# Feed-forward gate and up products by Strassen's scheme, with the down projection as a second phase

## What is computed

```python
def swiglu(h, wg, wu, wd):
    return (jax.nn.silu(h @ wg) * (h @ wu)) @ wd

x = x + g_m * rmsnorm(y, p['norm_mix_post'][l])          # y: the mixer's output projection
h = rmsnorm(x, p['norm_ffn_pre'][l]) * (1 + sc_f) + sh_f
f = swiglu(h, p['w_ffn_gate'][l], p['w_ffn_up'][l], p['w_ffn_down'][l])
x = x + g_f * rmsnorm(f, p['norm_ffn_post'][l])
```

## Time and profile before

| | |
|---|---|
| runs, us | 3237.58, 3239.43, 3239.88 (median 3239.43) |
| span of the profiled execution, us | 3236.1 |
| instructions | 63340 |
| busy share PE / PE weight load / DVE / ACT / POOL | 93% / 84% / 47% / 30% / 33% |
| DMA | 278.56 MB, mean 86 GB/s |
| tail of layer 0 | from 1042 to about 2036 us |
| tail of layer 1 | from 2273 us to the end |

### The profile page before, as it was taken

How to read it: one execution, slowest core, us unless ns; L and a number is a source line. 1 busy time by engine, 2 the same in 40 slices (tenths; PEclk the granted TensorE clock), 3 DMA queues, 4 the chain that set the end, 5 groups by cost and what they waited for, 6 DMA issues and landing times. The chain is left out here.

```text
span 3236.1 us, 63340 instructions
## 1 busy us (share of the span) xinstructions
PE 3020.7 (93%) x25847; PEld 2727.6 (84%) x25847; DVE 1534.6 (47%) x2856; ACT 958.8 (30%) x1871; POOL 1052.5 (33%) x693
## 2 busy tenths in 40 slices
PE   6999899889998989999999998898889999999997
PEld 4878576555556989999999997887889999999997
DVE  4332255555555573333333348787373333333336
ACT  5411146321112442111111126666452111111123
POOL 2410167433332532211212215675533112112212
PEclk8999989888889999999999999999999999999999
DMA  9555200355554222111111113201332111111103
GB/s 317 170 175 199 74 21 1 126 184 177 184 177 138 89 88 65 40 45 39 42 49 45 45 36 95 77 23 29 94 96 68 44 45 45 39 39 52 41 25 104
DMA packets 243842, 278.56 MB, mean 86 GB/s; under 512 B 13770, under 2 KB 191307, under 8 KB 243396
## 3 DMA queue, kind: packets, MB, share of 16 engines
q1 hardware_dynamic: 221500, 196.01, 19.4%
q0 software_dynamic: 20992, 75.51, 7.0%
q10 hardware_dynamic: 1168, 4.46, 0.4%
HBM read 249.69 MB, written 24.26 MB: 85 GB/s over the span
## 5 line engine op out<-in xcount | busy, mean ns | idle before, releaser
L564 PE MATMUL ps<-HS,w_ring 128*128 128x272 f32 x4992 | 643.4, 290 | 15.5 <-PEq L156 12.1
L564 PEld LDWEIGHTS ps<-HS,w_ring 128*128 128x128 f32 x4992 | 635.3, 189 | 16.8 <-POOLq L1071 12.3
L564 PE MATMUL ps<-HS,w_split 128*128 128x272 f32 x4608 | 593.0, 290 | 9.5 <-POOL w_split L1009 9.5
L564 PEld LDWEIGHTS ps<-HS,w_split 128*128 128x128 f32 x4608 | 587.1, 189 | 11.6 <-issue 7.6
L572 PE MATMUL ps<-hid,w_ring 128*128 128x272 f32 x4224 | 551.1, 291 | 3.5 <-DVE hid L1242 2.9
L572 PEld LDWEIGHTS ps<-hid,w_ring 128*128 128x128 f32 x4224 | 537.9, 189 | 7.6 <-DVE hid L1242 3.4
L1009 POOL TENSOR_TENSOR w_ring<-w_raw,w_ring 128x1024 fp32r<-128x1024 f32 x92 | 220.5, 2408 | 831.9 <-ACT w_ring L707 831.9
L1319 DVE TENSOR_TENSOR Y<-Y,ps 128x272 f32<-128x272 f32 x576 | 252.2, 438 | 176.7 <-PE ps L572 176.7
L1233 DVE TENSOR_TENSOR sg<-sg,ps 128x272 f32<-128x272 f32 x176 | 76.5, 437 | 382.4 <-ACT sg L818 382.3
L1853 PEld LDWEIGHTS ps<-HS_in,w_split 128*128 128x128 f32 x1728 | 222.2, 191 | 27.7 <-issue 16.4
L1853 PE MATMUL ps<-HS_in,w_split 128*128 128x272 f32 x1728 | 233.1, 293 | 9.2 <-DVE HS_in L2072 9.1
(11 more groups left out here) (413 smaller groups left out, 3882.2 us busy)
## 6 DMA issues: line engine op xcount, KB each, us to landing
w_mod_half<-w_mod_in SPq DMA_DIRECT2D x40, 1024.0 KB
w_raw<-w_ffn_gate_in SPq DMA_DIRECT2D x44, 512.0 KB
w_raw<-w_ffn_up_in SPq DMA_DIRECT2D x44, 512.0 KB, 3.7
w_raw<-w_ffn_down_in SPq DMA_DIRECT2D x44, 512.0 KB, 3.5
x_part<-x_spill SPq DMA_DIRECT2D x58, 272.0 KB, 2.9
x_spill<-Y SPq DMA_DIRECT2D x12, 1088.0 KB, 5.6
w_raw<-w_in_ab_in SPq DMA_DIRECT2D x18, 512.0 KB
w_raw<-w_in_cd_in SPq DMA_DIRECT2D x14, 512.0 KB, 3.9
```

The lines of the kernel that those rows point to most:

```text
L564: ins = pe.matmul(bank(b), wt[:, a, k, :], HS[:, e, k, qs(q)], start=(k == 0 and j == 0), stop=(k == KD - 1 and j == 2))
```

## The change

The token quarters are taken in two pairs (0 with 1, 2 with 3) and the 1024 features in two halves. For a pair, a hidden group of 256 columns and one matrix (gate or up), the product is a 2 x 2 by 2 x 2 block product, done in Winograd's form of Strassen's scheme: seven block products of 4 x 3 = 12 matmuls (`strassen`), called a unit, in place of the eight that four calls of `product` amount to.

- Weights: for each group and matrix, a batch, both column tiles arrive as two raw halves of 512 KB (`load_parts`). DVE makes four sums in place (`part_sum`), ACT seven high parts (`part_high`), POOL seven low parts (`part_low`), each 128 x 512. There is one slot for each part.
- Tokens: sums and differences of the blocks of `h` are made in `Y` in place (`token_sum`), and split like before (`token_high` on ACT, `token_low` on DVE), seven parts for each pair.
- Out of PSUM: a copy by ACT (`copy_a`), five additions by DVE (`add_b`, `add_e`, `add_22`, `add_12`, `add_21`), then the four sigmoids or high parts, multiplications and, for up, low parts.
- Order: groups 0 to 2 run on pair 0 alone, groups 3 to 10 on both pairs, then groups 0 to 2 on pair 1: 28 batches, 44 units. The work that the first loop did beside the first group (`first_beside`) lies beside units 0 to 6.
- Hidden activations, high and low, are stored to a DRAM scratch `hid_spill` (`store_hid`) and read back into `HS` (`load_hid`, `load_last`). The down projection runs after all units: four chunks of four hidden rows of 128 (12 matmuls for each of 32 banks), then a last one of six rows, quarter by quarter (18 matmuls), with the post norm beside it. The loops are written out.

In the units' code `u` is a unit, `m` its batch, `soon` that it is a batch's last unit and the batch has two, `late` that the batch has one. The diff, cut to the parts that set the order (`G` are three buffers of 272 columns, `finish` a sigmoid or a high part):

```diff
+KH = KD // 2
+SOLO = 3
+NCHUNK = 4
+DOWNS = 32 * NCHUNK
+NPROD = 7
+
+
+HALF_JOBS = ([(f, (0,)) for f in range(SOLO)] + [(f, (0, 1)) for f in range(SOLO, NFG)] + [(f, (1,)) for f in range(SOLO)])
+HALF_BATCH = [(f, mat, pairs) for f, pairs in HALF_JOBS for mat in range(2)]
+HALF_UNIT = [(m, f, mat, n) for m, (f, mat, pairs) in enumerate(HALF_BATCH) for n in pairs]
...
+DOWN_ROWS = [2 * f + i for c in range(NCHUNK) for f in (SOLO + 2 * c, SOLO + 2 * c + 1) for i in range(2)]
+DOWN_ROWS += [2 * f + i for f in range(SOLO) for i in range(2)]
...
+        def part_from(j):
+
+            low, high = slice(0, P), slice(P, 2 * P)
+            if j == 2:
+                return s1[:, :, :]
+            u, cols = {0: (0, low), 1: (0, low), 3: (1, low), 4: (0, high), 5: (1, low), 6: (1, high)}[j]
+            return part_raw[u][:, :, cols]
...
+        def load_hid(eng, k):
+
+            for i in range(4):
+                if i % 2 == 0:
+                    eng.wait_ge(hid_out, 32 * U.hid_stored(DOWN_ROWS[4 * k + i] // 2, (0, 1)))
+                base = 2 * Q * (k % 2)
+                src = hid_spill[DOWN_ROWS[4 * k + i]].rearrange("p a (h t) -> p a h t", h=2)
+                for a in range(2):
+                    eng.dma_start(HS[:, a, 2 * i:2 * i + 2, base:base + 2 * Q].bitcast(F32), src[:, a]).then_inc(hid_in[k % 2], 16)
...
+            def load_parts(m):
+                f, mat, pairs = U.BATCH[m]
+                src = w_cols((wg_d, wu_d)[mat], f * FG, FG)
+                if m == 0:
+                    sp.wait_ge(w_lo, 7)
+                else:
+                    sp.wait_ge(part_lo, NPROD * m)
+                for u in range(2):
+                    sp.dma_start(part_raw[u], src[:, KH * u:KH * u + KH, :]).then_inc(part_in[u], 16)
...
+            def store_hid(u):
+                m, f, mat, n = U.UNIT[u]
+                sp.wait_ge(hid_lo, 4 * U.ups(u) + 4)
+                dst = hid_spill[2 * f:2 * f + 2].rearrange("f p a t -> p a f t")[:, :, :, 2 * Q * n:2 * Q * n + 2 * Q]
+                for a in range(2):
+                    sp.dma_start(dst[:, a], hid[:, a].bitcast(F32)).then_inc(hid_out, 16)
...
+            def load_down(t):
+                if t < 2:
+                    sp.wait_ge(part_lo, NPROD * NBATCH)
+                else:
+                    sp.wait_ge(down_lo, t - 1)
+                apart(sp, sp_passed)
+                sp.dma_start(raw[t % 2][:, :], wd_d[DOWN_ROWS[t] * P:(DOWN_ROWS[t] + 1) * P, :]).then_inc(down_in[t % 2], 16)
...
+            for u in range(END):
+                m, f, mat, n = U.UNIT[u]
+                if u == U.FIRST[m] and m + 1 < NBATCH:
+                    load_parts(m + 1)
+                if u == 1:
+                    store_x(0, 3)
+                if u >= 1 and U.UNIT[u - 1][2]:
+                    store_hid(u - 1)
...
+            def strassen(u, j):
+
+                m, f, mat, n = U.UNIT[u]
+                b = (0, 1, 2, 0, 1, 2, 1)[j]
...
+                if j < 3 and u < 2:
+                    pe.wait_ge(freed_act, 4 * KD - NB6 + 3 * u + j + 1)
+                elif j == 0:
+                    pe.wait_ge(muls, 4 * (u - 2) + 1)
+                elif j == 1:
+                    pe.wait_ge(taken, 5 * (u - 2) + 5)
+                elif j == 2:
+                    pe.wait_ge(taken, 5 * (u - 2) + 4)
+                elif j == 3:
+                    pe.wait_ge(a_copied, u + 1)
+                else:
+                    pe.wait_ge(taken, 5 * u + j - 3)
+                pe.wait_ge(part_lo, NPROD * m + j + 1)
+                if u in (0, U.BOTH):
+                    pe.wait_ge(h_lo, NPROD * n + TOKEN_AT[j])
+                for k in range(KH):
+                    for i, (a, e) in enumerate(((0, 0), (0, 1), (1, 0))):
+                        ins = pe.matmul(psum(U.banks(u)[b]), part_slot(j, a)[:, k, :], token_part(n, j, e)[:, k, :],
+                                        start=(j < 3 and k == 0 and i == 0),
+                                        stop=(j in (3, 5, 6) and k == KH - 1 and i == 2), skip_group_check=True)
+                ins.then_inc(prod, 1)
+
...
+            for u in range(END):
+                for j in range(NPROD):
+                    strassen(u, j)
...
+            for k in range(NCHUNK):
+                pe.wait_ge(down_lo, 4 * k + 4)
+                pe.wait_ge(hid_in[k % 2], 128 * (k // 2 + 1))
...
+            def part_high(m, j):
+                if m == 0:
+                    act.wait_ge(computed, U.mix((3, 4, 4, 5, 5, 6, 6)[j], 3) + 1)
+                else:
+                    act.wait_ge(prod, NPROD * U.LAST[m - 1] + j + 1)
+                if j in (0, 3, 6):
+                    act.wait_ge(part_in[0 if j == 0 else 1], 16 * m + 16)
+                else:
+                    act.wait_ge(sums_made, 4 * m + {2: 1, 4: 2, 1: 3, 5: 4}[j])
...
+            def copy_a(u):
+                act.wait_ge(prod, NPROD * u + 1)
+                if u >= 1:
+                    act.wait_ge(muls, 4 * u)
+                act.activation(G[0], psum(U.banks(u)[0]), ACT.Copy).then_inc(a_copied, 1)
...
+            def half(u):
+                m, f, mat, n = U.UNIT[u]
+                more = u == U.LAST[m] and m + 1 < NBATCH
+                soon = more and not U.alone(m)
+                late = more and U.alone(m)
+
+                def finish(i):
+                    if mat:
+                        hidden_high(u, i)
+                    else:
+                        sigmoid(u, i)
+
+                copy_a(u)
+                if m and u == U.FIRST[m] and U.alone(m - 1):
+                    part_high(m, 5)
+                    part_high(m, 6)
+                first_beside(u, 0)
+                if soon:
+                    part_high(m + 1, 0)
+                    part_high(m + 1, 1)
+                    part_high(m + 1, 2)
+                    if mat:
+                        part_high(m + 1, 3)
+                        part_high(m + 1, 4)
+                finish(0)
+                first_beside(u, 1)
+                if late:
+                    part_high(m + 1, 0)
+                if soon and not mat:
+                    part_high(m + 1, 3)
+                first_beside(u, 2)
+                finish(1)
+                first_beside(u, 3)
+                if soon and not mat:
+                    part_high(m + 1, 4)
+                finish(2)
+                if late:
+                    part_high(m + 1, 1)
+                    part_high(m + 1, 2)
+                finish(3)
+                if late:
+                    part_high(m + 1, 3)
+                    part_high(m + 1, 4)
+                if soon:
+                    part_high(m + 1, 5)
+                    part_high(m + 1, 6)
+                first_beside(u, 4)
...
+            def down_high(t):
+                act.wait_ge(down_in[t % 2], 16 * (t // 2) + 16)
+                if t < 3:
...
+            for t in range(4):
+                down_high(t)
+            act.wait_ge(prod, NPROD * END)
+            load_hid(act, 1)
+            for t in range(4, 10):
...
+            def part_low(m, j):
+                pool.wait_ge(part_hi, NPROD * m + j + 1)
+                pool.tensor_tensor(part_slot(j, 1), part_from(j), part_slot(j, 0).bitcast(F32), ALU.subtract
+                                   ).then_inc(part_lo, 1)
...
+            def down_low(t):
+                w = slots[DOWN_SLOT[t]]
+                pool.wait_ge(down_hi, t + 1)
+                pool.tensor_tensor(w[:, 1, :], raw[t % 2][:, :], w[:, 0, :].bitcast(F32), ALU.subtract).then_inc(down_lo, 1)
...
+            def part_sum(m, j):
+                a11, a21 = part_from(0), part_from(4)
+                a12, a22 = part_from(3), part_from(6)
+                if j == 2:
+                    if m == 0:
+                        dve.wait_ge(computed, U.mix(3, 3) + 1)
+                    for u in range(2):
+                        dve.wait_ge(part_in[u], 16 * m + 16)
+                    ins = dve.tensor_tensor(s1[:, :, :], a21, a22, ALU.add)
+                elif j == 4:
+                    ins = dve.tensor_tensor(a21, a11, a21, ALU.subtract)
+                elif j == 1:
+                    dve.wait_ge(part_lo, NPROD * m + 1)
+                    dve.wait_ge(sums_made, 4 * m + 1)
+                    ins = dve.tensor_tensor(a11, s1[:, :, :], a11, ALU.subtract)
+                else:
+                    dve.wait_ge(part_lo, NPROD * m + 4)
+                    dve.wait_ge(sums_made, 4 * m + 3)
+                    ins = dve.tensor_tensor(a12, a12, a11, ALU.subtract)
+                ins.then_inc(sums_made, 1)
...
+            def add_b(u):
+                dve.wait_ge(prod, NPROD * u + 2)
+                dve.wait_ge(a_copied, u + 1)
+                dve.tensor_tensor(G[1], G[0], psum(U.banks(u)[1]), ALU.add).then_inc(taken, 1)
+
+            def add_e(u):
+                dve.wait_ge(prod, NPROD * u + 3)
+                dve.tensor_tensor(G[2], G[0], psum(U.banks(u)[2]), ALU.add).then_inc(taken, 1)
...
```

(37 more changed lines are left out.)

1332 lines of the change are left out of this document (706 added, 626 removed).

## The result

The changed kernel takes 3370.7 us (median of 4 runs, 3370.2 to 3371.3) and the kernel before 3239.6 beside it: ratio 1.0408, 95% interval 1.0393 to 1.0423, slower by 131 us. The forecast was 3361. The profiled execution has a span of 3369.1 us, 133.0 more than before.

A forecast was written before the change was run, and what follows sets the result against it. It took PE's matmul count to bound the kernel. Removed matmuls -132.6, supply loop +181, first units and mixer +24, double units +28, hidden-activation loads +6, hand-over +33, last quarters -18: +121.4, device time 3361 us, range 3200 to 3440.

The forecast's parts named there:

- matmuls removed: Gate and up products in both tails: 528 fewer matmuls a tail at 0.1256 us, -66.3 us each, -132.6 for two.
- mixer's last quarter: End of the mixer, DVE having 25 us of work beside 24 of PE: +2 us a tail.
- double units: Units while batches serve both token pairs: late sum 5 delays the next unit's `add_b` in up batches, +28 us in all.
- hand-over: From PE's last unit product to the down phase: waits for four low parts of weights, +16.5 us a tail, +33.
- last quarters: Last part of the down phase, now four even blocks of 18 us without sigmoids: -9 us a tail, -18.
- The supply loop: Units serving one pair: load waits for the previous batch's low parts; 18.8 us against 10.55, 22 times, +181.
- The shared access: DVE and POOL block each other on SBUF's shared ports: 2.3 us of the 18.8 us loop.
- Token work beside the first units: DVE and ACT token operations in each tail's first units, half hidden in the load wait: +10 us a tail.
- first rival: In units serving one pair, the reload is hidden well enough: loop 15.3 us, 3212 us total; chance 0.15.
- third rival: In units serving one pair, the loop runs at PE's pace because the load is early: 3180 us; chance 0.05.
- The slow clock: Stalls keep PE's clock low through units serving one pair: loop 21 us and more, 3447 us; chance 0.12.

The follow-up runs named there:

- The reorder: The mixer's third and fourth row sums issued later on PE, on the kernel where DVE makes low parts 3 and 6; ratio 1.0045 to the kernel before.
- the control: The changed kernel measured again, unaltered, on the chip of the follow-up runs; ratio 1.0420 to the kernel before, +132.0 us.

## Why the prediction was right, and where its sizes were off

Tail 0 by the prediction's own terms (stretches above, less 10.55 us a unit; before's stretches in the same way):

| term | predicted | measured |
|---|---|---|
| matmuls removed | -66.3 | -66.3 (by count) |
| units 0 to 6, less the 15.0 us that before lost in its first groups | +59.5 | +58.7 |
| last six units | +41.3 | +43.5 |
| mixer's last quarter | +2 | +12.1 |
| double units, `load_hid(0)` in them | +17 | +9.2 |
| hand-over | +16.5 | +16.0 |
| last quarters | -9 | -7 |
| sum | +61 | +66.2 |

**The bound and the matmuls.** Right where PE is fed. The run with the matmuls put back shows that in the single units they have no price, which the sum took in from the other side: it set each such unit at the loop's length.

The total is nearer than its terms. The two largest misses of a tail, +10.1 in the mixer and -7.8 in the double units, nearly cancel, and that is luck.

**The supply loop.** Right in its size: 18.4 us a unit late, for 18.8. The runs show the two things that it was built from, the load (4.7 and 3.9 us, priced 3.9) and the serial chain behind the landing. One step of that chain is missing from the prediction. It has sum 5 wait for low part 3; but sum 5 stands on DVE behind `add_b`, and in nine of the eleven single turns of tail 0 it starts straight behind `add_b`, 0.7 to 3.4 us after that low part is made. `add_b` waits for PE's second product, which takes 3.06 us at the slow clock in the turn shown, and for DVE's own queue (there four low parts, 4.73 us for 4 x 0.44 alone). No run parts the two. Nor are the chain's parts independent: of the three orders that start some of them earlier, two are slower beyond their intervals and none is faster.

**The shared access.** The sum priced it at 2.3 us a loop. The row of sum 5 beside POOL (1.27 for 0.68 us, so 0.6 of wait where the sum had 1.1) and 1.9 us a unit without that sum do not speak against it. The other way round it was priced too low: the four low parts of an up unit stand 4.73 us on DVE for 1.76 alone. The Trainium skill (SBUF — State Buffer, Who interferes with whom) calls the shared ports an exclusive lock and says that a DVE instruction with two SBUF inputs contends for them with a GpSimd (POOL) instruction that reads SBUF; these rows agree. But the access's share alone was not measured: two operations moved off POOL gave 0.7 us a late unit.

**Token work beside the first units.** Supply and token work together are met (+58.7 for +59.5), though with 15.0 us of old stalls taken off where the prediction named 8.5; no run gives the token work's own +10. It was wrong in kind: without the supply the first seven units lose 11.3 us, 8.5 of them in unit 0. The rest costs only when it shares DVE and ACT with the supply.

**The mixer's last quarter.** The term that was mis-sized: +2 for +12.1. "25 us of work beside 24 of PE" was read as a tie, but PE issues the third row sum ahead of its last 2 tiles, so DVE's lateness falls on it whole: 10.00 us. The kernel before has this row sum ahead of its last tile alone:

```profile
1148.68 0.73 PE L587 MATMUL ps<-squares_sum,ones 128*128 128x272 f32 x2 [1.39 <-DVE squares_sum L1183]
```

Counted from the mixer's first matmul the sum starts at 106.3 us before and at 113.1 after: 6.8 us of the 12.1 are lateness, and 5.3 come from the second tile behind the sum and from the slow clock (48 matmuls in 8.31 us there). The reorder shows that the time can't be had back by the place of the sum alone.

**The double units.** +17 for +9.2. The step named the wrong one in line: not the next unit's `add_b` behind the low parts, but `copy_a` behind the last multiplication behind sum 5, 0.75 us every fourth unit, about 5 of the 9.2. Where sum 5 stands later, that part is gone. `load_hid(0)`, priced at +3, shows as 2.0 in the last double unit (12.5 us): ACT issues its eight transfers ahead of `copy_a`, as forecast.

```profile
1634.88 4.52 ACTq L559 DMA_DIRECT2D HS<-hid_spill  x8
...
1639.95 1.76 PE L723 MATMUL ps<-HS,w_split 128*128 128x272 f32 x12 [1.65 <-ACT sg L963]
```

**The hand-over.** Right, 16.0 and 15.4 us. It is the load's second round and four low parts: with the loads ahead 8 us remain.

**The rivals.** The reload isn't hidden. With a second buffer for nine of the eleven it is, and the kernel is still slower than before, 1.0148, where the first rival's 3212 is under 1: its late units (13.6 us) are below the rival's 15.3, but the early ones take 19.2 on the mean, and the stalls of the mixer, the double units and the hand-over stay. The third rival is the run without the supply, 0.9739. The slow clock: the first products after a gap take 3.06 us for 1.67, near the lower of the clock's two levels (1.2 for 2.4 GHz), and the mean granted clock is 0.79 and 0.82 in the two bands; but by the fourth product of a unit it is back, mostly by the third, and without the supply the same units run at 10.5. So the slow clock follows from the gaps and doesn't keep the units long by itself. What it adds to the loop through the second product and `add_b` was not measured.

What stays open: how the remaining 13.6 us of a late unit, and 19 of an early one, divide between the access, ACT's order, DVE's order and the slow clock of the second product.

## What to carry to other kernels

Count what a scheme needs per weight as well as what it saves per product. Here a batch of seven parts costs POOL and DVE the same whether it serves one token pair or two; for two it is hidden, for one it isn't, and 22 of 88 units lost some 200 us against 133 saved. A loop through load, ACT, DVE and POOL, in which PE is busy 66% and 73% and no other engine over 63%, is found by following one buffer round, not by busy shares; the cure that paid was room (a second buffer, weights loaded ahead), never another order alone, except where a sum stood ahead of work that the next unit waits for.

## What the runs showed of the hardware

The same changed kernel is 106 us shorter on the control's chip than on the first, and all of it lies ahead of unit 0 of tail 0 (1055.34 for 1162.27), in the attention over the pages, which the change doesn't touch: from its first matmul (L3025) to its last 420.3 us pass on the one and 314.3 on the other. Stretch 600 to 800, and the stage's largest group over its whole length, first chip and then the control's:

```profile
600.00:800.00 200.00, 177.20 (x2648) 115.02 (x2656) 109.52 (x188) 36.25 (x59) 74.61 (x76) 0.87 0.58 188
```

```profile
L3025 PE MATMUL ps<-k_all,q_rows 32*64 32x256 f32 x2304 | 122.3, 449 | 26.0 <-issue 16.8 <-PEq L156 7.5
```

```profile
600.00:800.00 200.00, 180.70 (x3638) 134.78 (x3640) 150.95 (x257) 48.37 (x80) 96.89 (x100) 0.97 0.76 247
```

```profile
L3025 PE MATMUL ps<-k_all,q_rows 32*64 32x256 f32 x2304 | 72.2, 388 | 18.1 <-issue 9.5 <-PEq L156 7.7 <-DVE k_all L2563 0.8
```

The granted clock is 0.87 on the one and 0.97 on the other, one matmul takes 449 and 388 ns on the mean (the median is 374 on both), and in the same 200 us PE gets through 2648 and 3638 matmuls, the DMAs through 188 and 247 GB/s. The clock alone is 12%, the stage takes 34% longer on the first chip; what else differs between the chips the runs don't show. Times of different chips can't be compared here; ratios can: 1.0408 and 1.0420.
